# A two-layer hybrid encoder trunk: first score tiles moved into the stages before, transposed weighing, new orders at stage ends

## The reference

```python
for i in range(DEPTH):
    h = _rmsnorm(x, g_pre[i])
    o = _even_mixer(...) if i % 2 == 0 else _odd_mixer(...)
    x = x + _rmsnorm(o, g_post[i])
    x = x + jax.nn.sigmoid(x @ w_ple_gate[i]) * (p[i] @ w_ple[i])
```

## Time and profile before

| | us |
|---|---|
| median of 3 runs (lowest, highest) | 1870.07 (1866.65, 1872.04) |
| the profiled execution's own time | 1868.86 |
| its span in the profile | 1867.1 |
| DVE busy | 1310.4 (70%) |
| ACT busy | 801.6 (43%) |
| POOL busy | 823.0 (44%) |
| matmul instructions | 9736 |

### The profile page before, as it was taken

The page is one execution under the profiler, slowest core; times in us unless marked ns, Lnnn a source line. Parts: engine busy times, 40 slices in busy tenths (PEclk is TensorE's granted clock), DMA queues, the critical chain, the costliest instruction groups (busy, mean ns, idle before and its releaser), DMA issues. The chain is left out here.

```text
span 1867.1 us, 27184 instructions
## 1 busy us (share of the span) xinstructions
PE 1829.6 (98%) x9736; PEld 1556.9 (83%) x9736; DVE 1310.4 (70%) x2151; ACT 801.6 (43%) x1581; POOL 823.0 (44%) x568
## 2 busy tenths in 40 slices
PE   6999999999999999999999999999999999999999
PEld 5788888888799888878888888887898898888887
DVE  3598999826688425632679957666777777778886
ACT  6211212211488432211254544432788787445432
POOL 2231233222488563375645341213887983444211
PEclk9999999999999999999999999999999999999999
DMA  5122555443487556565433353594446459658744
GB/s 206 46 68 96 193 160 177 166 149 125 128 285 241 178 189 222 179 209 186 156 111 119 122 168 91 191 355 154 143 159 226 157 176 376 201 177 292 248 147 141
DMA packets 160108, 331.94 MB, mean 178 GB/s; under 512 B 32690, under 2 KB 66226, under 8 KB 159987
## 3 DMA queue, kind: packets, MB, share of 16 engines
q1 hardware_dynamic: 159986, 330.36, 52.6%
HBM read 207.63 MB, written 122.68 MB: 177 GB/s over the span
## 5 line engine op out<-in xcount | busy, mean ns | idle before, releaser
L191 POOL TENSOR_TENSOR w_lo_part<-w_raw,w_hi_part 128x1024 fp32r<-128x1024 f32 x56 | 137.7, 2467 | 338.3 <-ACT w_hi_part L183 338.2
L615 DVE SCALAR_TENSOR_TENSOR ie_ps<-ie_u,ie_wconv,ie_ps 128x1024 f32<-128x1024 f32 x240 | 225.2, 1012 | 0.0
L3492 PE MATMUL og_ps<-w_hi_part,bl_ring 128*128 128x512 f32 x672 | 217.7, 394 | 1.0 <-DVE bl_ring L3025 1.0
L246 PE MATMUL ie_ps<-rows_hi,w_hi_part 128*128 128x512 f32 x384 | 150.8, 393 | 0.0
L246 PE MATMUL ie_ps<-rows_hi,w_lo_part 128*128 128x512 f32 x384 | 149.8, 390 | 0.0
L3492 PEld LDWEIGHTS og_ps<-w_hi_part,bl_ring 128*128 128x128 f32 x672 | 127.0, 189 | 27.1 <-DVE bl_ring L3025 1.1
L246 PE MATMUL ie_ps<-rows_lo,w_hi_part 128*128 128x512 f32 x384 | 149.7, 390 | 0.0
L2913 DVE TENSOR_TENSOR mla_pt_lo<-mla_ps_t,mla_pt_hi 128x512 fp32r<-128x512 f32 x160 | 108.9, 686 | 33.5 <-ACT mla_pt_hi L2882 32.5
L3492 PE MATMUL og_ps<-w_lo_part,bl_ring 128*128 128x512 f32 x336 | 131.5, 391 | 0.0
L2882 ACT CAST mla_pt_hi<-mla_ps_t 128x512 fp32r<-128x512 f32 x160 | 94.1, 592 | 53.5 <-PE mla_ps_t L2833 49.7
L2906 DVE TENSOR_REDUCE mla_min<-mla_ps_s 128x1 f32<-128x1024 f32 (+1 forms) x96 | 100.0, 1042 | 21.9 <-PE mla_ps_s L2823 20.7
(11 more groups left out here) (359 smaller groups left out, 5174.5 us busy)
## 6 DMA issues: line engine op xcount, KB each, us to landing
w_raw<-wall SPq DMA_DIRECT2D x62, 512.0 KB, 4.8
w_hi_part<-weight_blocks SPq DMA_DIRECT2D x28, 512.0 KB, 4.8
w_lo_part<-weight_blocks SPq DMA_DIRECT2D x28, 512.0 KB, 5.8
weight_blocks<-w_hi_part SPq DMA_DIRECT2D x26, 512.0 KB, 6.6
w_raw_tiles<-wall SPq DMA_DIRECT2D x16, 512.0 KB, 5.2
odd_sums<-w_raw_tiles SPq DMA_DIRECT2D x8, 1024.0 KB, 4.4
w_raw<-odd_sums SPq DMA_DIRECT2D x16, 512.0 KB, 4.2
w_flat<-wall SPq DMA_DIRECT2D x16, 512.0 KB, 8.8
```

The lines of the kernel that those rows point to most:

```text
L191: pool.tensor_tensor(g.W[1][:, pair % 2, off:off + QCOLS], g.raw[:, n % 2, :], g.W[0][:, pair % 2, off:off + QCOLS].bitcast(F32), ALU.subt ...
L246: mm = pe.matmul(psum[:, u % banks], w_at(g, name, a, k * HALF + c * P, P), g.XT[m][:, k, b * 512:(b + 1) * 512], start=i == 0, stop=i == ...
L615: dve.scalar_tensor_tensor(out, ubuf[:, cc, at.start + s:at.stop + s], wconv[:, cc, s:s + 1], out, ALU.mult, ALU.add).then_inc(taps, 1)
L3492: mm = pe.matmul(ps[:, N % 4], bl.part(a, N)[:, k], wb.at(N // HT, m, k), start=k + a + m == 0, stop=k == 3 and a == 1)
```

## The change

It touches all stages.

- in_even: POOL scales the first four tiles' statistics in two steps; DVE scales tiles 0 to 2 and ACT tile 3; PE transposes tiles 0 and 1 of four groups, then 2 and 3. The third block's rows are scaled just ahead of `rows_low(14)`. DVE's last step of a layer-normed tile moves into the next tile's wait for POOL.
- natten: the first three score tiles, their minima and exponents stand in in_even's last unit (two ahead of its products, one behind). `weigh` holds the transposed weights stationary and moves V, so the result is not transposed; ACT scales the low half, DVE scales the high half and adds. `turn_back`, its copy, its PSUM bank and the load of the folding matrix go; the weighing bank is doubled.
- out_proj: `turn_main(0)` stands in the middle of the third `side_half`. gate: gate products run one further ahead up to unit 8. in_odd: two entries are combined one unit earlier.
- latent_fnet: the sign row becomes an fp32r product over 128 partitions (high row 0, low row 32, zeros elsewhere); `S` has two buffers; gate tiles lie elsewhere and the second is loaded behind the first head's operands.
- mla: its first two score tiles, minima and exponents stand in the last channel group, and that group's two mixes behind mla's steps 3 and 5. The second head's load moves ahead of mla, and POOL's work there waits for those mixes.
- out_and_gate: the first two blocks are split two (ACT) and four (DVE) steps earlier.

```diff
+        def first_scale(t):
+            pool.wait_ge(squared, t + 2)
+            rms_scale(pool, g, ss[:, t:t + 2], D, scaling, t)
...
-        scale_of(0)
-        pool.wait_ge(scaled, 4)
+        first_scale(0)
+        first_scale(2)
+        pool.wait_ge(scaled, 3)
...
-        for n in range(3):
+        first_high(0)
+        act.wait_ge(scaling, 4)
+        act.activation(x_at(3), x_at(3), ACT.Copy, scale=ss[:, 3:4]).then_inc(last_scaled, 1)
+        for n in range(1, 3):
...
+            if u == U - 1:
+                for j in range(2):
+                    na.exponents(act, j)
...
+        na.exponents(act, 2)
...
+            for t in range(4 * b, 4 * b + (4 if b else 3)):
+                dve.wait_ge(scaling, 2 * (b + 2) if b else 2 * (t // 2 + 1))
...
+        def finish(t):
+            y = yb[t % 3]
+            dve.wait_ge(y_tanhed, t + 1)
+            dve.scalar_tensor_tensor(y, thy, 1.0, y, ALU.add, ALU.mult).then_inc(urow, 1)
...
+            if t:
+                finish(t - 1)
...
-            dve.wait_ge(y_tanhed, t + 1)
-            dve.scalar_tensor_tensor(y, thy, 1.0, y, ALU.add, ALU.mult).then_inc(urow, 1)
...
+            if u == Y0 + NT:
+                finish(NT - 1)
...
+                    if v == 14:
+                        scale_rows(2)
...
-            if u == 3:
-                scale_rows(2)
...
+                if u == U - 1:
+                    for j in range(na.FIRST):
+                        na.minimum(dve, banks[:, j % 2], j)
...
+            pe.wait_ge(scaled, 4 * b + min(tiles[-1] + 1, 3))
+            if tiles[-1] == 3:
+                pe.wait_ge(last_scaled, 1)
...
+            if u == U - 1:
+                for j in range(2):
+                    pe.wait_ge(ev_dve, by_dve[U - 3 + j])
+                    na.products(pe, banks[:, j], j)
...
-        for v in range(4):
-            turn_group(v)
+        for tiles in (range(2), range(2, 4)):
+            for v in range(4):
+                turn_group(v, tiles)
...
+        pe.wait_ge(na.minned, 1)
+        na.products(pe, banks[:, 0], 2)
...
+    def products(self, pe, bank, j):
...
+        pe.matmul(dst, self.Q1[:, q:q + P], keys, start=True, stop=False)
+        pe.matmul(dst, self.Q2[:, q:q + P], keys, start=False, stop=True).then_inc(self.scored, 1)
...
+    def minimum(self, dve, bank, j):
...
+        dve.tensor_tensor_reduce(self.S[:, j, 0:n], bank[:, 0:n], self.xt[:, COLTYPE[NA_TILE[j][1]], P:3 * P], -1.0, 3e38, ALU.add, ALU.min,
+                                 self.mins[:, j:j + 1]).then_inc(self.minned, 1)
...
+    def exponents(self, act, j):
...
+        act.activation(self.S[:, j, 0:n], self.S[:, j, 0:n], ACT.Exp, bias=self.mins[:, j:j + 1], scale=-1.0,
+                       accum_out=self.sums[:, j // 2, j % 2:j % 2 + 1]).then_inc(self.exped, 1)
...
-                if u >= 1:
-                    pe.wait_ge(copied, u)
+                if u >= 2:
+                    pe.wait_ge(normed, u - 1)
...
+                for a in range(2):
+                    first = 6 * (i - 2) + a if prompt(u) else 6 * (2 * i + a) + 4
                     for part in range(2):
-                        for rb in (1, 2):
-                            pe.matmul(both, v(cw, rb), PT[part][:, u % 2, rb:rb + 3:2], start=part == 0 and rb == 1, stop=part == 1 and rb == 2)
-                    for part in range(2):
-                        pe.matmul(ps_pv[:, 0:P], v(cw, 0), PT[part][:, u % 2, 0], start=False, stop=False, skip_group_check=True)
-                        mm = pe.matmul(ps_pv[:, P:2 * P], v(cw, 3), PT[part][:, u % 2, 5], start=False, stop=part == 1, skip_group_check=True)
-                else:
-                    for a in range(2):
-                        for part in range(2):
-                            for c in range(2):
-                                mm = pe.matmul(ps_pv[:, a * P:(a + 1) * P], v(2 * i + a, 4 + c), PT[part][:, u % 2, 2 * a + c],
-                                               start=a + part + c == 0, stop=part + c == 2, skip_group_check=True)
+                        for c in range(n):
+                            mm = pe.matmul(ps_pv[:, u % 2, a * P:(a + 1) * P], PT[part][:, u % 2, a * n + c], V[:, h % 2, first + c],
+                                           start=part + c == 0, stop=part == 1 and c == n - 1)
                 mm.then_inc(weighed, 1)
...
-                else:
-                    pe.wait_ge(normed, u)
+            for u in range(NPAIRS + 3):
                 for a in range(2):
-                    mm = pe.matmul(ps_back[:, a * DH:(a + 1) * DH], pv_sb[:, u % 2, a * P:(a + 1) * P], fold[:], start=True, stop=True)
-                mm.then_inc(back, 1)
...
-            def copy(u):
+            def scale_low(u):
                 act.wait_ge(weighed, u + 1)
+                act.wait_ge(inverted, u + 1)
                 if u >= 2:
-                    act.wait_ge(back, u - 1)
-                act.copy(pv_sb[:, u % 2], ps_pv[:, 0:256]).then_inc(copied, 1)
+                    act.wait_ge(normed, u - 1)
+                for a in range(2):
+                    done = act.activation(pv_lo[:, u % 2, a], weighted(u, a, 1), ACT.Copy, scale=rinv[:, u % 3, a:a + 1])
+                done.then_inc(scaled, 1)
 
...
+            def invert(u):
+                dve.wait_ge(exped, 2 * u + 2)
+                if u >= 3:
+                    dve.wait_ge(normed, u - 2)
+                dve.reciprocal(rinv[:, u % 3], sums[:, u % NA_U]).then_inc(inverted, 1)
...
-                dve.reciprocal(rinv[:, u % 2], sums[:, u % NA_U]).then_inc(inverted, 1)
-                dve.wait_ge(back, u + 1)
-                dve.wait_ge(inverted, u + 1)
+                dve.wait_ge(scaled, u + 1)
...
-                t0, t1 = NA_QPOS[2 * i], NA_QPOS[2 * i + 1]
-                dve.tensor_tensor(out[:, hp % 2, t0:t1 + 1:t1 - t0, h % 2 * DH:h % 2 * DH + DH],
-                                  ps_back[:, 0:P].rearrange("p (a d) -> p a d", a=2),
-                                  rinv[:, u % 2].rearrange("p (a o) -> p a o", o=1).broadcast_to([P, 2, DH]),
-                                  ALU.mult).then_inc(normed, 1)
+                for a in range(2):
+                    done = dve.scalar_tensor_tensor(out[:, hp % 2, NA_QPOS[2 * i + a], h % 2 * DH:h % 2 * DH + DH], weighted(u, a, 0),
+                                                    rinv[:, u % 3, a:a + 1], pv_lo[:, u % 2, a], ALU.mult, ALU.add)
+                done.then_inc(normed, 1)
...
-                products(0, t, range(4), False)
+                products(0, t, range(2), False)
+                if t == LEAD - 1:
+                    turn_main(0)
+                products(0, t, range(2, 4), False)
...
-            turn_main(0)
...
+        U, AHEAD = 2 * NT, 8
...
             for u in range(U):
-                if u == 2:
-                    gate_products(3)
-                if u >= 4:
+                if 2 <= u < AHEAD:
+                    gate_products(u + 1)
+                elif u > AHEAD:
                     gate_products(u)
                 embedding(u)
...
-        return ODD_G1 + 8 * (b - 1) + (4 + j // 2 if j < 4 else 8)
+        return ODD_G1 + 8 * (b - 1) + (4 if j < 4 else 8)
...
+class FirstScores:
...
+    def products(self, pe, bank, t, s):
...
+    def exponents(self, act, bank, j):
...
-    yh = g.region(end).sb("fn_y_half", [1, 2, P])
+    yh = g.region(end).sb("fn_y_half", [P, 2, P], F32R)
...
+    S2 = [g.region(at).sb(f"fn_s{i}", [P, TOK]) for i, at in enumerate((ml.end - 4 * TOK, ml.end + 8192))]
+    ps_fn = st.enter_context(nc.psum_tensor("fn_ps", [P, 4, HALF], F32))
+    ps_y, ps_yh, ps_half = ps_fn[:, 0:2], ps_fn[:, 2], ps_fn[:, 3]
+    first_bank = lambda j: ps_fn[:, 2 * j:2 * j + 2].rearrange("p a c -> p (a c)")
...
+            else:
+                sp.wait_ge(y_mm, (ROUNDS + 1) * c + ROUNDS)
...
-        load_gate(1)
         ml.load_rope(g, sp)
         ml.load(g, sp, 0, slice(0, DH))
+        load_gate(1)
...
-        for done in g.fnet_out:
-            sp.wait_ge(*done)
+            if c == 2:
+                sp.wait_ge(ml.prepped, ml.PREPS)
+                ml.load(g, sp, 1, slice(DH, 2 * DH))
...
+        def half_rows_low(c):
...
+                dve.scalar_tensor_tensor(yh[low, i], ps_yh[low, i * P:(i + 1) * P], 0.5 * (n * P) ** -0.5, yh[low, i].bitcast(F32),
+                                         ALU.mult, ALU.subtract).then_inc(yh_lo, 1)
...
-                if r == 2 and c:
-                    mix(c - 1, 0)
-                    mix(c - 1, 1)
                 if c + 1 < NGR:
                     low(c + 1, r)
+            last = c + 1 == NGR
+            if c:
+                mix(c - 1, 0)
+            if last:
+                mix(c - 1, 1)
             for i in range(2):
+                if last:
+                    dve.wait_ge(fs.pl["scored"], i + 1)
+                    fs.reduce(dve, first_bank(i), i)
                 unfold(c, i)
-        mix(NGR - 1, 0)
-        mix(NGR - 1, 1)
```

(40 more changed lines are left out.)

225 lines of the change are left out of this document (120 added, 105 removed).

## The result

The changed kernel takes 1857.93 us (median of 4 runs, 1854.9 to 1860.07) against 1870.47 for the kernel before: ratio 0.994 [0.9926, 0.9953]. That is faster by 12.5 us, where 23.2 were forecast, and 0.9 us above the range.

What follows compares the result with a forecast made beforehand. The prediction took PE, busy 98% of the span, as the bound, plus the chain feeding each stage's successor. Eleven terms summed to 23.2 us, so 1868.9 - 23.2 = 1845.7 us, with a range of 1836 to 1857.

Steps and rivals of the forecast that it cites:

- third block's rows: In in_even: scaling ahead of `rows_low(14)` removes PE's late transpose start, -1.8 us (-1.4 to -1.8).
- Rival 2: In latent_fnet, waiting for POOL's operands and DVE's mixes takes most of both gains: 5.0 shrinks to 1.5, 1849.2 us; chance 0.13.
- Rival 3: In natten, weight loads bound the weighing: +32.5 us, 1882.2, chance 0.02; milder form 1872.5, chance 0.03.
- Rival 1: ACT and DVE take PE's place in natten, so the 4.0 us go: 1849.7 us; chance 0.17.
- term of -4.0: natten's weighing: fewer PE matmuls without the turn back, -4.0 us (0 to -8.0).
- natten's start: Three score tiles ready early fill part of 1.99 us idle at natten's start: -1.4 us (0 to -2.0).
- Layer-normed units: In in_even, deferring DVE's 0.69 us step brings its round from 6.63 to 5.24: -2.1 us (-1.8 to -2.1).
- Sign row and mla's first tiles: In latent_fnet and mla: cheaper sign products, -2.9 us net of waits; mla's starting wait gone, -2.1 us.
- natten's end: Last units and out_proj's first product no longer wait 0.87 and 0.96 us: -2.0 us (-0.3 to -2.8).
- out_and_gate: At its start, 0.98 us of wait goes and no half clock is expected: -2.5 us (-0.5 to -2.5).
- in_even's start: Transposes of tiles 0 and 1 lie beside the last two scalings: -1.0 us (0 to -2).
- Rival 4: Whole kernel: behind each removed wait stands the next, leaving half of every gain, 1857.3 us; chance 0.10.

Runs made afterwards that it cites:

- experiment 1: The changed kernel, but ACT takes a unit's gate tanh before the layer-normed tile's tanh: 1848.78 us, ratio 0.9883.
- experiment 3: The changed kernel, but natten's first three score tiles stand in natten again: 1850.2 us, ratio 0.9894.
- Experiment 7: The changed kernel, but mla computes its first two score tiles itself, as before: 1853.16 us, ratio 0.9918.
- experiment 8: The changed kernel with ACT's gate tanh first, V prepared last, mla's first tile behind the group's first token products, eight weight loads behind gate rows: 1845.18, again 1843.89 us.
- experiment 4: The kernel before with only the new weighing (V moved, no turn back), natten's first tiles staying in natten: 1866.12 us over 8 runs, ratio 0.9975.
- experiment 2: The changed kernel, but DVE finishes each layer-normed tile at once, as before: 1856.65 us, ratio 0.9925.

## Why the prediction was wrong, and where it was right

Right in kind: PE's order is serial, gains add up by stretch, and three of the eleven terms came out within 0.2 (third block's rows, gate, in_odd). So did the clock behind mla at 1.00, which with the 0.98 of the earlier trace rows gave -2.6 up to that point. Rival 2's wait came too, larger than priced. Rival 3 is out: in PE's timeline of the change a prompt unit's weighing starts, and the next scores start, at

```profile
557.57 0.53 PE L1087 MATMUL na_ps_pv<-na_v,na_pt_hi 128*128 128x128 f32 x3
558.94 0.34 PE L1057 MATMUL na_ps_s<-w_hi_part 128*128 128x256 f32 x1
```

that is 1.37 us for 12 matmuls, 0.114 each, as the earlier trace rows let expect. Rival 1 is out for the later heads: ACT and DVE rise to 106.34 and 103.52 of 116, below PE's 113.89, since a 64-column activation takes 318 ns and a DVE operation 276 (by line and form; minimum, median and maximum in ns):

```profile
L1121 ACT ACTIVATE na_pv_lo<-na_ps_pv,na_rinv x96: 307/318/341, 507.0 to 623.0; 128x64 f32<-128x64 f32 x96
L1170 DVE SCALAR_TENSOR_TENSOR na_out<-na_ps_pv,na_rinv,na_pv_lo x96: 273/276/285, 508.7 to 623.5; 128x64 f32<-128x64 f32 x96
```

So the term of -4.0 was too cautious, though not by as much as the later heads promise. These take 14.7 us instead of 15.57; eight of them would give some 7. The first three, counted from a head's first transposes to the next one's, give 0.8 together (14.39, 15.22 and 14.98 where 13.89, 15.94 and 15.56 stood), with PE waiting 0.2 to 0.6 at a time for DVE's low parts in the first two, which speaks for rival 1 in small. Measured are 5.0 from natten's first transposes to its end.

What failed, in order of size:

1. **natten's start, -1.4 (0 to -2.0); measured +8.4 by in_even's end, +6.1 by natten's first transposes.** The prediction looked at who reads the early tiles (the third minimum, the first weighing), not at what the tiles themselves wait for. The second tile's bank is freed by DVE's gate of a unit two earlier, DVE reaches that gate some 5 us after PE asks for it, and in_even's last products queue behind the tile: 5.1 idle, 2.6 lost at half clock behind it and 0.5 for the tiles' own products make the 8.4 up to 0.2. No bound of the term allowed a loss. Experiments 1 and 3 show it from both sides.
2. **Layer-normed units, -2.1; measured -0.4.** "Deferring the 0.69 step fills POOL's wait and drops the other" took the step's time from a stretch without POOL (0.69, it became 1.24) and didn't follow ACT's order, where the dropped wait came back ahead of the gate. With ACT's order mended the same stretch gives -2.3 (experiment 1): the size was right, the order it needs was missing.
3. **Sign row and mla's first tiles, -5.0; measured -2.25.** The wait for POOL was foreseen and mis-sized: 1.5 forecast, 5.1 measured, and the half clock behind it wasn't counted. Counted from in_odd's end, PE reached the last group's first tile 5.7 us earlier and not 4, and POOL's operands came 0.3 earlier (1280.54 for 1286.95) and not 2: the last load that POOL waits for, V's, is issued 60 us behind in_odd's end in both kernels. Without the tiles PE wins 8.7 up to mla's first weighing (the change 3.3), more than forecast. The sign row's term was too small: from one channel group's sign row to the next it takes 10.6 us instead of 12.5, 1.9 less, where 5.4 / 4 = 1.35 was forecast. That of the tiles had the wrong sign as built. And what the prediction put at nothing, the second head's operands, costs 1.0: POOL prepares them behind the last mix, and PE waits 0.72 for the last of them (1322.26 above), a wait that every version with the change shows and the kernel before doesn't.
4. **natten's end, -2.0; measured +1.0.** The order did what it should; the half clock in the tail took it back. Experiment 7 shows this without meaning to: its code is the same up to there, its profile has the clock at 1.00 in the tail, and from natten's last transposes to gate's first product it wins the forecast's 2.0 us, where the change loses 1.2. It is no single case: of the ten profiles of the change and its variants without unread products in the tail, five have the half clock there and lose 1.2 to 1.4 us in that stretch, and five have 1.00 and win 2.0 to 2.2.
5. **out_and_gate, -2.5; measured -1.0.** The prediction didn't ask what is late next. It is the gate rows, queued on SP behind the weights' loads; experiment 8 shows that by its order.

in_even's start went the other way (-2.6 for -1.0): PE's transposes begin at 9.26 instead of 15.33. But the other profiles with the same start have -0.6 to -2.5 there, and experiment 4's, with the start of the kernel before, -1.5: one profile doesn't size a term this small.

Rival 4 named the measured time almost to the microsecond (1857.3), by luck and not for its reason. Half of *each* gain was not lost; most came in full, and a few new waits, two of them followed by the half clock, took back more than the rest.

What stays open: whether the tail's clock falls for the short waits. The count of 9 of 9 against 5 of 12 speaks for it; but the kernel before waits longer at its natten's end (0.87) and its profile shows 1.00 there.

## What to carry to other kernels

Work that is moved ahead on PE brings its own waits along: for each of its semaphores find the engine that signals it, and how far behind PE that engine runs at the new place, before counting what the move hides. A wait of some 5 us on PE cost about half as much again behind it (2.6 and 2.2 us), at half clock, so a sum that prices only the wait is too low; and a wait that one engine's order has moved can sit two lines further on in another's.

## What the hardware showed that I had not expected

- The granted clock in natten's tail differs between executions of one kernel (0.50 and 1.00 over the same 8 us, experiment 8), 3.5 us apart from natten's last transposes to gate's first product. The Trainium skill ("TensorE: Matmul & The Clock Gate", section "What's actually happening") says that the number of matmuls at the low clock, from a kernel's start, varies from run to run of the same kernel; here it does in the middle of one.
- A DVE step with two SBUF inputs took 1238 ns beside POOL instead of 693, and POOL's one-column step 513 instead of 192; both went back when experiment 2 moved them apart.
- All 512 matmuls of the new weighing have weights of their own and at full clock still start some 0.11 us apart, though a load's record lasts 0.19.
